# Pool columns of a hybrid layer computed channel by token, in groups of 512 tokens

## The chip, the cores and the metric

One Trainium2 chip, one core in use. The metric is the device time of the program in microseconds (us); lower is better. Every number is a time of an execution on the chip or is read from the trace of one such execution.

## The reference, cut to what matters

One layer on 1024 tokens of width 1024, all float32:

```python
h = rms_norm(x, norm1_g)
u, q, k, v = split(h @ w_in)             # 512 | 512 | 128 | 128 columns
# pool mixer: 4 channel groups of 128, windows 2, 4, 8, 16 tokens
pooled[g] = trailing_mean(u[g], window[g]) - u[g]
a[g] = (pooled[g] @ pool_w[g]) * pool_scale[g]
# attention: 8 query heads, 2 key heads of 64, window of 128 tokens in chunks of 64,
# q and k normed per head, a bias linear in distance, a sink term in the softmax
b = attention(q, k, v)
x = x + concat(a, b) @ w_out
x = x + square(relu(rms_norm(x, norm2_g) @ w_up)) @ w_down
```

## The kernel before, in words

Each engine has its own program, written out by hand, and runs it strictly in its order; engines meet through semaphores. Tokens come in 8 tiles of 128 (t). A float32 matrix product is made of three fp32r products: each operand is split into a rounded high part (ScalarE, `..._high`, `split_...`) and the rest as a low part (VectorE, `..._low`), and `passes` (L1250) issues high x high, high x low and low x high. x comes transposed; the norm's row factor `rinv` is applied later, when a product leaves PSUM, as one scalar per token, since tokens lie on the partitions.

**Input projection.** `project_in(t, ks)` (L1269) takes eight steps k of 128 rows of w_in. In each step the token tile is the stationary operand, and it issues nine matmuls: three of 256 columns (k and v, bank 2), three of 512 (q, bank 3), three of 512 (u, bank 4). In tile 0 each waits for the split of its w_in columns; later ones wait only for bank 2, 3, 4 to have been copied. The w_in rows come as 8 transfers of 640 KB through 6 staging buffers.

**Per tile, after the projection.** ScalarE copies k and v, q and u out (`copy_kv` L637, `copy_q` L647, `copy_u` L654) with `rinv` as scale. GpSimd squares q and k, VectorE sums (`head_sums`), GpSimd takes the inverse root, VectorE norms (`head_norm` L962). TensorE's `transpose_in(t)` (L1322) turns u (four transposes), then q (four) and k (one). The tile `qkv` is single, so `copy_kv(t)` waits for `transpose_in(t-1)`. `evac_u` and `evac_qk` (ScalarE) bring the results to SBUF. GpSimd adds windows over the four groups (`window_sums` L491), VectorE finishes the mean (`pooled` L935), `mix(t)` (L1345) multiplies in plain float32 by pool_w, one matmul per group, `mix_high` and `mix_low` write the halves of a into `xs`, whose x values are no longer needed.

**Attention.** `score(t)` (L1356) writes banks 5 and 6; `softmax_head`, `exponentials`, `softmax_tail` work on VectorE and ScalarE; `transpose_probs(t)` (L1338) writes the transposed probabilities back into banks 5 and 6, `evac_probs` (L682) copies them out in two instructions, and only then may `score(t+1)` write these banks (its wait on `pT_copied`); `attend(t)` (L1373) uses bank 7.

**TensorE's order** (L1389 to L1423): for each t, part of `project_in(t)`, `transpose_in(t-1)`, the rest of `project_in(t)`, `transpose_probs(t-2)`, `mix(t-1)`, `score(t-1)`, `attend(t-2)`. Then `project_out` (L1297) over w_out, eight steps per tile of six matmuls of 512, with the last attention pieces between, `transpose_x` of the second norm, and the MLP (`up`, `down`), whose seven products per block replace eight.

w_out is loaded into the space of w_in's split parts while these fall free, through 5 staging buffers.

Of the kernel before, what the change touches and what calls it, by code (L numbers as in the profile page):

```python
# [11 lines left out]
P = 128  # L12
BANK = 512
# [3 lines left out]
def hybrid_trunk(nc, x, x_T, columns, w_in, pool_w, w_out, norm2_g, w_up, w_down, out):  # L17
# [26 lines left out]
    w_in_k = w_in[0].rearrange("(k p) e -> k p e", p=P)  # L44
    w_out_k = w_out[0].rearrange("(k p) n -> k p n", p=P)
    w_up_k = w_up[0].rearrange("(k p) f -> p k f", p=P)
    w_down_i = w_down[0].rearrange("(j i p) n -> i p j n", i=2, p=P)
    x1_keep = nc.dram_tensor("x1_keep", [NT, P, D], F32, kind="Internal").ap()
    h_keep = nc.dram_tensor("h_keep", [7, NCK, P, HALF], F32, kind="Internal").ap()

    with ExitStack() as ctx:
# [22 lines left out]
        w_in_s = wgt[:, :].rearrange("p (k h e) -> p k h e", k=KT, h=2)  # L74
# [12 lines left out]
        def view(a, words):  # L87
# [3 lines left out]
        UB = HALO + P  # L91
        a_x = take(2 * D)
        a_A = take(2 * D)
        a_B = take(4 * D)
        a_C = take(3 * D)
        a_ws = take(2 * D)
        a_xn = take(D)
        a_bp = take(D)
        a_junk = take(D // 2)
        xT_slot = [view(a_x + i * D, D).rearrange("p (k n) -> p k n", k=KT) for i in range(2)]  # L100
        u_tok = view(a_A, POOL_W)
        qkv = view(a_A + POOL_W, Q_W + KV_W)
        squares = view(a_A + POOL_W + Q_W + KV_W, Q_W + P)
# [3 lines left out]
        u_T = view(b, GROUPS * UB).rearrange("p (g s) -> p g s", g=GROUPS); b += GROUPS * UB  # L107
        win_a = view(b, GROUPS * UB).rearrange("p (g s) -> p g s", g=GROUPS); b += GROUPS * UB
        win_b = view(b, 3 * UB).rearrange("p (g s) -> p g s", g=3); b += 3 * UB
        assert b <= a_B + 4 * D  # L110
        scores = [view(a_C + i * BANK, BANK).rearrange("p (t j) -> p t j", t=PAIRS) for i in range(2)]
        probs_T = [view(a_C + D + i * BANK, BANK) for i in range(2)]
        values = view(a_C + 2 * D, 8 * P).rearrange("p (r c n) -> p r c n", r=4, c=2)
# [3 lines left out]
        pool_map = view(a_bp + BANK, BANK).rearrange("p (g n) -> p g n", g=GROUPS)  # L117
        junk = view(a_junk, D // 2).bitcast(BF16)

        w_in_stage = ([view(a_C + i * IN_W, IN_W) for i in range(2)] + [view(a_A, IN_W)]  # L120
                      + [view(a_B + i * IN_W, IN_W) for i in range(3)])
        w_out_stage = [view(a, D) for a in (a_ws, a_ws + D, a_x, a_x + D, a_xn)]
        W_OUT_SLOT = [0, 1, 2, 3, 4, 0, 1, 4]
        dist = view(a_ws, P)

        resid = ([view(a_x + i * D, D) for i in range(2)] + [view(a_A + i * D, D) for i in range(2)]
                 + [view(a_B + i * D, D) for i in range(4)])
# [37 lines left out]
        KV_B, Q_B, U_B = 2, 3, 4  # L165
        XT_B = [[5, 6], [1, 7]]
        UT_B, QT_B, KT_B = 0, 1, 7
        MIX_B, SC_B, OUT_B = 0, [5, 6], 7
        TOK_B = [2, 3, 4, 0]

# [6 lines left out]
        w_in_in = [sem(f"w_in_in{i}") for i in range(6)]  # L177
        w_out_in = [sem(f"w_out_in{i}") for i in range(5)]
# [4 lines left out]
        d_in = {q: [sem(f"d_in_{q}_{i}") for i in range(8)] for q in ("B11", "B12", "B22", "B21")}  # L183
# [9 lines left out]
        w_in_hi, w_in_lo = sem("w_in_hi"), sem("w_in_lo")  # L193
        rows_hi, rows_lo = sem("rows_hi"), sem("rows_lo")

        in_done = sem("in_done")
        kv_done, q_done = sem("kv_done"), sem("q_done")
        kv_copied, q_copied, u_copied = sem("kv_copied"), sem("q_copied"), sem("u_copied")
# [3 lines left out]
        uT_done, qT_done, kT_done = sem("uT_done"), sem("qT_done"), sem("kT_done")  # L202
        halo_ready, u_T_ready, q_T_ready, keys_ready = sem("halo_ready"), sem("u_T_ready"), sem("q_T_ready"), sem("keys_ready")

        win_step, pool_step, pooled_ready = sem("win_step"), sem("pool_step"), sem("pooled_ready")
        mix_done, mix_hi, mix_lo = sem("mix_done"), sem("mix_hi"), sem("mix_lo")
# [19 lines left out]
        KV_COLS, Q_COLS, U_COLS = slice(POOL_W + Q_W, IN_W), slice(POOL_W, POOL_W + Q_W), slice(0, POOL_W)  # L226
        PIECES = {0: (KV_COLS, Q_COLS, U_COLS), 1: (slice(POOL_W, IN_W), U_COLS)}

        def w_pieces(k):
            return PIECES.get(k, (slice(0, IN_W),))  # L230

        def w_count(k, cols=U_COLS):

            done = sum(len(w_pieces(j)) for j in range(k))
            return done + 1 + min(i for i, c in enumerate(w_pieces(k)) if c.start <= cols.start and cols.stop <= c.stop)
# [57 lines left out]
        def _(sp):  # L293
# [10 lines left out]
            def load_w_in(k):  # L304
                if k >= 6:
                    sp.wait_ge(w_in_lo, w_count(k - 6))
                sp.dma_start(w_in_stage[k % 6], w_in_k[k]).then_inc(w_in_in[k % 6], 16)

            def load_w_out(k):
                slot = W_OUT_SLOT[k]  # L310
                if slot in W_OUT_SLOT[:k]:
                    sp.wait_ge(rows_lo, W_OUT_SLOT.index(slot) + 1)
# [52 lines left out]
            for k in range(6):  # L365
                load_w_in(k)
            load_x(0)
            load_w_in(6)
            load_w_in(7)
            load_xT(1)  # L370
            sp.dma_start(pool_map, pool_w).then_inc(pool_map_in, 16)
            for t in range(1, NT):
                if t + 1 < NT:
                    load_xT(t + 1)
                load_x(t)
            sp.wait_ge(setup_done, 4)
            load_w_out(0)
            load_w_out(1)
            sp.wait_ge(xT_lo, 2 * (NT - 1))
            load_w_out(2)  # L380
            sp.wait_ge(xT_lo, 2 * NT)
            load_w_out(3)
            sp.wait_ge(sumsq_ready, NT)
            load_w_out(4)
            for k in range(5, KT):
                load_w_out(k)
            sp.wait_ge(in_done, KT * NT)
            load_raw(1)
# [12 lines left out]
            for t in range(4, NT):  # L401
                sp.dma_start(resid[t], x_t[ORDER[t]]).then_inc(resid_in[t], 16)
# [63 lines left out]
        def _(pool):  # L466
# [1050 lines left out]
```

## Time and profile before

| | us |
|---|---|
| median of 3 runs | 874.14 (873.89 to 874.4) |
| the profiled execution, its own time | 874.23 |
| its span in the trace | 871.8 |
| TensorE busy | 863.9 |
| VectorE busy | 531.8 |
| ScalarE busy | 418.5 |
| GpSimd busy | 269.9 |

The span runs from the first to the last recorded instruction; the 2.4 us between it and the execution's time lie around it. A matmul's record lasts longer than the distance to the next one, since matmuls overlap in the array: what it costs is the distance of the starts. The part up to the first transpose of the second norm (L1265) ends at 189.56 us of the span.

### The profile page before, as it was taken

Reading aid. Unit: us, or ns where it says so; the run is one execution under the profiler, and the core shown is the slowest. Engines: PE = TensorE matmul, PEld = TensorE weight load, DVE = VectorE, ACT = ScalarE, POOL = GpSimd, SP = SyncE. Lnnn points to the kernel's source line nnn. Section 1 sums busy time; section 2 is a strip of 40 time slices with the busy share of each in tenths; the row PEclk is TensorE's granted clock in tenths of the full one; section 3 lists DMA queues with packets and bytes.
Section 4 is the critical chain, followed back from the end, with each engine's and each line's share of the span. In section 5 each row is a group of like instructions: output and inputs, shape, how many; then the busy total and the mean of one; then the engine's idle time right before and its main releaser. Section 6 shows DMA issues by size and latency. Waiting matters only on the chain.

```text
span 871.8 us, 10957 instructions
## 1 busy us (share of the span) xinstructions
PE 863.9 (99%) x4128; PEld 715.8 (82%) x4128; DVE 531.8 (61%) x800; ACT 418.5 (48%) x746; POOL 269.9 (31%) x202
## 2 busy tenths in 40 slices
PE   8999999999999999999999999999999999999998
PEld 6888888788888888888888888888888888888886
DVE  7666558944458676567666666466945464646462
ACT  7566658632236655555555555444333333333330
POOL 0633444300231342222333222104544004444440
PEclk9999999999999999999999999999999999999999
DMA  8311232452111564444555442889752553242421
GB/s 350 122 49 49 90 105 49 170 180 86 49 48 35 191 194 161 133 134 133 171 178 158 157 133 85 301 319 390 252 184 97 169 193 120 96 147 97 145 97 73
DMA packets 66340, 128.38 MB, mean 147 GB/s; under 512 B 3568, under 2 KB 19952, under 8 KB 66288
## 3 DMA queue, kind: packets, MB, share of 16 engines
q1 hardware_dynamic: 66144, 127.68, 42.6%
q8 instruction: 33, 0.54, 0.2%
q14 instruction: 19, 0.16, 0.1%
q10 hardware_dynamic: 144, 0.01, 0.0%
HBM read 89.92 MB, written 37.75 MB: 146 GB/s over the span
## 4 chain that ended last, share of the span: by engine, by line
PE 89%; DVE 5%; DMA 2%; ACT 2%; POOL 1%; issue 1%; SPq 0%; ACTq 0%; DVEq 0%; POOLq 0%
PE bank L1252 28%; PE bank L1254 28%; PE bank L1253 28%; DMA mem<-in_w_in 2%; PE bank L1367 1%; DVE ring L1033 1%; PE bank L1265 1%; PE bank L1352 1%; PE bank L1382 1%; POOL mem L504 1%; DMA raw<-in_w_up 1%; PE bank L1342 1%; DVE wgt L932 1%; DVE h_set L1065 1%; DVE t_M L1041 1%
## 5 line engine op out<-in xcount | busy, mean ns | idle before, releaser
L1252 PE MATMUL bank<-b_op,s_op 128*128 128x512 f32 x448 | 174.6, 390 | 0.0
L1254 PE MATMUL bank<-b_op,s_op 128*128 128x512 f32 x448 | 174.5, 390 | 0.0
L1253 PE MATMUL bank<-b_op,s_op 128*128 128x512 f32 x448 | 174.5, 390 | 0.0
L572 POOL TENSOR_TENSOR b_sum<-d_raw,d_raw 128x1024 f32<-128x1024 f32 x40 | 97.7, 2442 | 199.8 <-DVE b_op L1076 199.8
L1072 DVE TENSOR_TENSOR s_op<-s_in,s_op 128x1024 fp32r<-128x1024 f32 x56 | 75.0, 1338 | 124.8 <-ACT s_op L775 124.8
L775 ACT ACTIVATE s_op<-s_in 128x1024 fp32r<-128x1024 f32 x56 | 59.4, 1060 | 177.7 <-PE bank L1254 147.1
L1252 PE MATMUL bank<-wgt,xs 128*128 128x256 f32 (+1 forms) x320 | 121.1, 378 | 1.8 <-DVE wgt L926 1.5
L1253 PE MATMUL bank<-wgt,xs 128*128 128x256 f32 (+1 forms) x320 | 118.4, 370 | 0.0
L1254 PE MATMUL bank<-wgt,xs 128*128 128x256 f32 (+1 forms) x320 | 118.3, 370 | 0.0
L1033 DVE TENSOR_TENSOR ring<-raw,ring 128x512 fp32r<-128x512 f32 x96 | 88.8, 938 | 31.0 <-ACT ring L723 29.5
L1252 PE MATMUL bank<-xs,ring 128*128 128x512 f32 x256 | 99.9, 390 | 0.1
L1254 PE MATMUL bank<-xs,ring 128*128 128x512 f32 x256 | 99.8, 390 | 0.0
L1253 PE MATMUL bank<-xs,ring 128*128 128x512 f32 x256 | 99.7, 390 | 0.0
L1252 PEld LDWEIGHTS bank<-b_op,s_op 128*128 128x128 f32 x448 | 84.1, 188 | 17.9 <-DVE b_op L1076 0.4
L1253 PEld LDWEIGHTS bank<-b_op,s_op 128*128 128x128 f32 x448 | 84.1, 188 | 17.4
L1254 PEld LDWEIGHTS bank<-b_op,s_op 128*128 128x128 f32 x448 | 84.1, 188 | 17.3
L538 POOL TENSOR_TENSOR raw<-raw 128x512 f32<-128x512 f32 x16 | 26.2, 1640 | 167.2 <-DVE ring L1033 167.0
L1252 PE MATMUL bank<-t_M,ring 128*128 128x512 f32 x192 | 74.9, 390 | 0.1
L1254 PE MATMUL bank<-t_M,ring 128*128 128x512 f32 x192 | 74.8, 390 | 0.0
L1253 PE MATMUL bank<-t_M,ring 128*128 128x512 f32 x192 | 74.8, 389 | 0.0
L1252 PEld LDWEIGHTS bank<-wgt,xs 128*128 128x128 f32 x320 | 60.3, 188 | 16.4 <-issue 4.0
L723 ACT ACTIVATE ring<-raw 128x512 fp32r<-128x512 f32 x96 | 59.3, 620 | 25.2 <-POOL raw L538 22.7
(129 smaller groups left out, 1358.2 us busy)
## 6 DMA issues: line engine op xcount, KB each, us to landing
s_in<-h_keep SPq DMA_DIRECT2D x56, 512.0 KB, 3.9
h_keep<-h_set SPq DMA_DIRECT2D x16, 1280.0 KB, 5.1
raw<-in_w_up SPq DMA_DIRECT2D x16, 1024.0 KB, 6.4
d_raw<-in_w_down SPq DMA_DIRECT2D x32, 512.0 KB, 7.7
mem<-in_x SPq DMA_DIRECT2D x16, 512.0 KB, 5.7
h_keep<-h_set SPq DMA_DIRECT2D x16, 512.0 KB, 3.8
mem<-in_w_in SPq DMA_DIRECT2D x8, 640.0 KB, 8.0
mem<-in_x_T SPq DMA_DIRECT2D x8, 512.0 KB, 3.8
```

What stands on the lines that cost most here:

```text
L504: nc.gpsimd.tensor_tensor(out=dst[:, d0:d0 + cnt, lo:UB], in0=src[:, s0:s0 + cnt, lo:UB], in1=src[:, s0:s0 + cnt, lo - shift:UB - shift], ...
L538: nc.gpsimd.tensor_tensor(out=w12, in0=w12, in1=w11, op=ALU.subtract).then_inc(w_four_ready, 1)
L572: nc.gpsimd.tensor_tensor(out=b_sum[G % 2], in0=group_rows(qa, g), in1=group_rows(qb, g), op=op).then_inc(b_summed, 1)
L723: nc.scalar.activation(ring[n % 6][:, HI], weight_block(n), ACT.Copy).then_inc(w_hi, 1)
L775: nc.scalar.activation(s_op[G % 3][:, HI], s_in[G % 3], ACT.Copy).then_inc(op_hi, 1)
L932: nc.vector.tensor_tensor(out=w_out_s[:, k, LO, :], in0=w_out_stage[W_OUT_SLOT[k]], in1=w_out_s[:, k, HI, :].bitcast(F32), op=ALU.subtract ...
L1033: nc.vector.tensor_tensor(out=ring[n % 6][:, LO], in0=weight_block(n), in1=ring[n % 6][:, HI].bitcast(F32), op=ALU.subtract).then_inc(w_lo, 1)
L1041: nc.vector.tensor_tensor(out=lo, in0=src, in1=hi.bitcast(F32), op=ALU.subtract).then_inc(t_lo, 1)
L1072: nc.vector.tensor_tensor(out=s_op[G % 3][:, LO], in0=s_in[G % 3], in1=s_op[G % 3][:, HI].bitcast(F32), op=ALU.subtract).then_inc(op_lo, 1)
L1252: nc.tensor.matmul(out_ap, lhs[HI], rhs[HI], start=first, stop=False, skip_group_check=chained)
L1253: nc.tensor.matmul(out_ap, lhs[HI], rhs[LO], start=False, stop=False, skip_group_check=chained)
L1254: return nc.tensor.matmul(out_ap, lhs[LO], rhs[HI], start=False, stop=last, skip_group_check=chained)
```

## The change

The columns of w_in are treated in two parts. The k, v and q columns (768) keep their scheme: `project_qkv(t, ks)`, six matmuls per step. The u columns are computed with the weights as the stationary operand and 512 tokens (h = 0 or 1) as the moving one, one channel group g at a time: `project_u(h, g)`, 24 matmuls of 512 columns, so that u leaves the array already as channel by token. The row factor now lies along the free axis: `rinv` goes through DRAM and comes back as a row on all partitions, and VectorE multiplies by it (`scale_u`). Window sums, mean and mix run per (h, g) on 512 tokens. The pooled values and pool_w are split in high and low parts, and `mix(h, g)` is three fp32r matmuls of 512 columns. u and mix use banks 4 and 0 alternately. w_in arrives as 8 transfers of 384 KB (q, k, v columns) and, behind x and x_T, 4 of 512 KB (u columns); w_out has 3 staging buffers in place of 5.

```diff
             def project_qkv(t, ks):
...
+                    elif first:
                         pe.wait_ge(kv_copied, t)
+                        pe.wait_ge(q_copied, t)
...
+            def project_u(h, g):
+                n = GROUPS * h + g
+                cols = slice(g * P, (g + 1) * P)
+                pe.wait_ge(xT_lo, 2 * KH * (h + 1))
+                if g >= 2:
+                    pe.wait_ge(u_ready, n - 1)
+                elif h:
+                    pe.wait_ge(mix_lo, GROUPS * (h - 1) + g + 3)
+                for k in range(KT):
+                    if n == 0:
+                        pe.wait_ge(w_u_lo, k + 1)
+                    last = passes(bank[U_B[g % 2]][:, :], [w_u_s[:, k, part, cols] for part in (HI, LO)],
+                                  [xs[k // KH, h][:, part, k % KH, :] for part in (HI, LO)], k == 0, k == KT - 1)
+                last.then_inc(u_done, 1)
...
+            def mix(h, g):
+                n = GROUPS * h + g
+                pe.wait_ge(pooled_lo, n + 1)
+                if n == 0:
+                    pe.wait_ge(map_lo, 1)
+                if g < 2:
+                    pe.wait_ge(u_ready, GROUPS * h + g + 3)
+                else:
+                    pe.wait_ge(mix_lo, n - 1)
+                last = passes(bank[U_B[g % 2]][:, :], [pool_map[:, part, cols] for part in (HI, LO)],
+                              [pooled_part(h, g)[:, part, :] for part in (HI, LO)], True, True)
...
 # TensorE's order, one line per stretch; project_qkv(t) whole unless steps are given
+ project_qkv(0)  project_qkv(1)  transpose_in(0)
+ project_qkv(2, 0..3)  score(0)  project_qkv(2, 4..7)  transpose_in(1)
+ project_u(0,0)  project_u(0,1)  transpose_probs(0)  score(1)  attend(0)
+ project_qkv(3)  transpose_in(2)  project_u(0,2)  project_u(0,3)  transpose_probs(1)  score(2)  attend(1)
+ project_qkv(4, 0..3)  mix(0,0)  mix(0,1)  project_qkv(4, 4..7)  transpose_in(3)
+ mix(0,2)  mix(0,3)  transpose_probs(2)  score(3)  attend(2)
+ project_u(1,0)  project_qkv(5)  transpose_in(4)
+ project_u(1,1)  project_u(1,2)  transpose_probs(3)  score(4)  attend(3)
+ project_u(1,3)  project_qkv(6, 0..3)  transpose_in(5)  project_qkv(6, 4..7)
+ transpose_probs(4)  score(5)  attend(4)  project_qkv(7)  transpose_in(6)
+ mix(1,0)  mix(1,1)  project_out(0, 0..2)  mix(1,2)  mix(1,3)
+ transpose_probs(5)  score(6)  attend(5)  project_out(0, 3..5)  transpose_in(7)  project_out(0, 6..7)
+ project_out(1, 0..1)  transpose_probs(6)  score(7)  attend(6)  project_out(1, 2..7)  project_out(2, 0..1)
+ transpose_probs(7)  project_out(2, 2..3)  attend(7)  transpose_x(8)  project_out(2, 4..7)
 # ScalarE's order in the stretches that the prediction walks through
+ split_w_qkv(0..7)  sum_squares_x(0)  x_high(1)  split_w_u(0..3)  copy_kv(0)  copy_q(0)
+ x_high(2)  sum_squares_x(1)  split_w_u(4..7)  evac_qk(0)  copy_kv(1)  copy_q(1)
...
+ x_high(7)  attention_high(0)  evac_probs(1)  sum_squares_x(7)  pooled_high(0,0)  exponentials(2)
+ pooled_high(0,1)  attention_high(1)  mix_high(0,0)  mix_high(0,1)  pooled_high(0,2)  pooled_high(0,3)
+ evac_qk(3)  copy_kv(4)  copy_q(4)  mix_high(0,2)  evac_probs(2)  mix_high(0,3)
...
+ evac_qk(5)  split_w_out(0)  split_w_out(1)  copy_kv(6)  copy_q(6)  split_w_out(2)  evac_probs(4)
+ split_w_out(3)  attention_high(4)  exponentials(5)  pooled_high(1,1)  split_w_out(4)  split_w_out(5)
+ evac_qk(6)  copy_kv(7)  copy_q(7)  mix_high(1,0)
 # VectorE's, likewise
+ place_values(0)  head_sums(0)  x_low(2)  split_w_u(4..7)  head_norm(0)
...
+ scale_u(0,3)  attention_low(0)  softmax_head(2)  pooled_low(0,0)  pooled(0,2)  softmax_tail(2)  pooled_low(0,1)
...
+ softmax_head(5)  split_w_out(3)  attention_low(4)  softmax_tail(5)  pooled(1,3)  pooled_low(1,1)
```

In `pooled_high(1, g)` with odd g ScalarE waits for all eight `pooled`. SyncE loads, in this order: x_T of tile 0, the eight q, k, v parts, x of tile 0, x_T of tile 1, two u parts, x_T of tile 2, x of tile 1, two u parts, x_T of tile 3, x of tile 2, and so on. From `transpose_x` on only the places of some buffers differ, and the third `project_out` has four steps left there in place of five.

## Rows read from the trace of the kernel before

**Rows 1.** Page: busy time per engine, and TensorE's granted clock in 40 slices.
```profile
PE 863.9 (99%) x4128; PEld 715.8 (82%) x4128; DVE 531.8 (61%) x800; ACT 418.5 (48%) x746; POOL 269.9 (31%) x202
PEclk9999999999999999999999999999999999999999
```
**Rows 2.** Page: the chain that ended last, shares of the span by engine.
```profile
PE 89%; DVE 5%; DMA 2%; ACT 2%; POOL 1%; issue 1%; SPq 0%; ACTq 0%; DVEq 0%; POOLq 0%
```
**Rows 3.** Waits of TensorE past tile 0: total us, times, longest.
```profile
PE bank L1332 <- DVE mem L966: 0.6, 1, 0.6
PE bank L1342 <- DVE mem L1003: 0.4, 1, 0.4
```
**Rows 4.** Timeline of TensorE, first 50 us: start, duration, instruction, count.
```profile
1.55 4.88 PE L1388 MATMUL bank<-mem 128*128 128x128 f32 x24 [1.55 <-POOL mem L471]
7.49 0.35 PE L1252 MATMUL bank<-wgt,xs 128*128 128x256 f32 x1 [1.06 <-DVE wgt L926]
...
23.52 0.28 PE L1252 MATMUL bank<-wgt,xs 128*128 128x256 f32 x1
...
25.31 0.28 PE L1252 MATMUL bank<-wgt,xs 128*128 128x256 f32 x1
...
27.05 0.28 PE L1252 MATMUL bank<-wgt,xs 128*128 128x256 f32 x1
...
30.54 0.60 PE L1328 MATMUL bank<-mem 128*128 128x128 f32 x4
30.98 0.60 PE L1332 MATMUL bank<-mem 128*128 128x128 f32 x4
...
38.49 1.05 PE L1352 MATMUL bank<-mem 128*128 128x128 f32 x8
39.47 1.16 PE L1367 MATMUL bank<-mem 64*128 64x128 f32 x16
```
**Rows 5.** Timeline of all engines, 130 to 137 us, same columns.
```profile
131.52 1.04 PE L1342 MATMUL bank<-mem 128*128 128x128 f32 x8
...
132.16 1.09 ACT L687 ACTIVATE mem<-bank 128x512 f32<-128x512 f32 x2 [0.45 <-PE bank L1342]
...
132.40 1.06 PE L1352 MATMUL bank<-mem 128*128 128x128 f32 x8
```
**Rows 6.** Timeline of ScalarE, 14 to 19 us.
```profile
14.10 1.37 ACT L624 ACTIVATE wgt<-mem 128x1280 fp32r<-128x1280 f32 x1 [0.23 <-DMA mem<-in_w_in]
...
16.95 1.37 ACT L624 ACTIVATE wgt<-mem 128x1280 fp32r<-128x1280 f32 x1 [1.49 <-DMA mem<-in_w_in]
```
**Rows 7.** Groups of ScalarE by form, 0 to 210 us: busy, mean ns | idle before.
```profile
L705 ACT ACTIVATE mem<-mem 128x128 f32<-128x128 f32 x64 | 25.0, 391 | 15.2 <-DVE mem L987 15.2
...
L587 ACT ACTIVATE mem<-mem 128x1024 bf16<-128x1024 f32 x11 | 11.5, 1049 | 12.6 <-DVE mem L1024 9.5 <-DMA mem<-in_x 3.1
L600 ACT ACTIVATE xs<-mem 128x512 fp32r<-128x512 f32 x16 | 9.2, 617 | 2.2 <-DMA mem<-in_x_T 2.2
...
L631 ACT ACTIVATE wgt<-mem 128x1024 fp32r<-128x1024 f32 x8 | 8.1, 1056 | 1.0 <-DMA mem<-in_w_out 1.0
...
L650 ACT ACTIVATE mem<-bank,mem 128x512 f32<-128x512 f32 x8 | 5.5, 687 | 0.4
...
L644 ACT ACTIVATE mem<-bank,mem 128x256 f32<-128x256 f32 x8 | 3.8, 472 | 19.6 <-PE bank L1254 18.9 <-POOL mem L488 0.7
...
L679 ACT ACTIVATE mem<-bank,mem 128x128 f32<-128x128 f32 x8 | 2.9, 367 | 0.0
...
L624 ACT ACTIVATE wgt<-mem 128x512 fp32r<-128x512 f32 x3 | 2.0, 708 | 0.0
```
**Rows 8.** Groups of VectorE by form, 0 to 210 us.
```profile
L1003 DVE TENSOR_SCALAR mem<-mem 128x128 f32<-128x128 f32 x64 | 14.1, 283 | 0.6
...
L985 DVE TENSOR_REDUCE mem<-mem 128x4 f32<-128x512 f32 x16 | 11.0, 686 | 0.6
...
L983 DVE TENSOR_TENSOR mem<-bank,mem 128x512 f32<-128x512 f32 x14 | 9.6, 685 | 3.4 <-PE bank L1367 3.4
```

More of the change, by code:

```diff
@@ new lines, in _ @@
+            exponentials(3)
+            evac_qk(4)
+            copy_kv(5)
+            copy_q(5)
+            evac_probs(3)
+            attention_high(3)
+            exponentials(4, (0,))
+            pooled_high(1, 0)
+            exponentials(4, (1,))
+            evac_qk(5)
+            for k in range(2):
+                split_w_out(k)
+            copy_kv(6)
+            copy_q(6)
+            split_w_out(2)
+            evac_probs(4)
+            split_w_out(3)
+            attention_high(4)
@@ new lines, in _ @@
+            exponentials(5)
+            pooled_high(1, 1)
+            for k in range(4, 6):
+                split_w_out(k)
+            evac_qk(6)
+            copy_kv(7)
+            copy_q(7)
+            mix_high(1, 0)
+            mix_high(1, 1)
+            pooled_high(1, 2)
+            pooled_high(1, 3)
+            split_w_out(6)
+            evac_probs(5)
+            mix_high(1, 2)
+            mix_high(1, 3)
+            attention_high(5)
+            exponentials(6, (0,))
+            split_w_out(7)
@@ new lines, in _ @@
+            scale_u(1, 0)
+            place_values(5)
+            head_sums(5)
+            head_norm(5)
+            scale_u(1, 1)
+            pooled(1, 0)
+            scale_u(1, 2)
+            softmax_head(4)
+            attention_low(3)
+            softmax_tail(4)
+            pooled(1, 1)
+            scale_u(1, 3)
+            pooled_low(1, 0)
+            pooled(1, 2)
+            for k in range(2):
+                split_w_out(k)
+            place_values(6)
+            head_sums(6)
@@ new lines, in _ @@
+            split_w_out(2)
+            head_norm(6)
+            softmax_head(5)
+            split_w_out(3)
+            attention_low(4)
+            softmax_tail(5)
+            pooled(1, 3)
+            pooled_low(1, 1)
+            for k in range(4, 6):
+                split_w_out(k)
+            place_values(7)
+            head_sums(7)
+            mix_low(1, 0)
+            mix_low(1, 1)
+            pooled_low(1, 2)
+            pooled_low(1, 3)
+            head_norm(7)
+            split_w_out(6)
@@ new lines, in _ @@
+            mix(0, 0)
+            mix(0, 1)
+            project_qkv(4, range(KH, KT))
+            transpose_in(3)
+            mix(0, 2)
+            mix(0, 3)
+            transpose_probs(2)
+            score(3)
+            attend(2)
+            project_u(1, 0)
+            project_qkv(5, range(KT))
+            transpose_in(4)
+            project_u(1, 1)
+            project_u(1, 2)
+            transpose_probs(3)
+            score(4)
+            attend(3)
+            project_u(1, 3)
```

735 lines of the change are left out of this document (430 added, 305 removed).

## The prediction

> **What bounds the kernel now.** Read the page first: TensorE is busy in 99% of the span, the next engine in 61%, and the granted clock is full in every slice [rows 1]. The chain of waits agrees: 89% of it is TensorE [rows 2]. TensorE's waits past the first tile come to 0.6 and 0.4 us [rows 3]. So the time is TensorE's own work, and an edit is worth what it takes out of TensorE's queue, less each wait that it puts there. In the timeline a tile's projection is 15 units of 256 columns per step; from 25.31 to 27.05 that is 1.74 us, 0.116 us a unit, 0.232 us for a matmul of 512 [rows 4]. The profiled execution (874.23) is the median of the runs (874.14); the sum is made on it, and the 2.4 us around the span stay.
>
> **TensorE's work.** Removed: the u transposes, four in 0.44 us per tile (30.54 to 30.98), 8 x 0.44 = 3.5; the float32 mix, 0.98 us per tile (38.49 to 39.47), 8 x 0.98 = 7.8 [rows 4]. The two old waits go with the order, 1.0 [rows 3]. Added: 8 mixes of three matmuls of 512, 24 x 0.232 = 5.6. The u product is 192 matmuls of 512 columns before and after; weights instead of tokens as the stationary operand change no count of columns. It could stream a little better or worse (I hold 0.005 us each, 1 us in all, for both ends) and I take 0. Together: -3.5 - 7.8 + 5.6 - 1.0 = **-6.7 us**.
>
> **Start: weights in two parts.** Before, tile 0 ends at 23.52 [rows 4] for 8 x 1.74 = 13.9 of work: it lags its work by 9.6. In the new order `project_qkv(1)` waits for `copy_q(0)`, and ScalarE comes to this only behind four splits of u weights. Loads: between 14.10 and 16.95 x (512 KB) and w_in's step 6 (640 KB) land, 404 KB per us; by 14.10, 4352 KB have landed [rows 6]. Two u parts are complete after 512 + 8 x 384 + 4 x 512 = 5632 KB, so at 14.1 + 1280/404 = 17.3. Then two splits (0.7 each, less overlap: 18.6), `copy_kv` 0.47, `copy_q` 0.69 [rows 7]: 19.8. By then TensorE has done 8 x 1.04 = 8.3 of work, finished near 16.2, and stands for 3.6. It lags by 11.5 instead of 9.6: **+1.9**. Ends: -1.8 (no stand at all), +4 (the loads drop to the bandwidth of smaller rows).
>
> **After `project_qkv(1)`.** `transpose_in(0)` follows at once, then `project_qkv(2)`, which needs banks 2 and 3 copied. ScalarE can copy only after `evac_qk(0)`: 0.69 (a copy of 512 columns from PSUM, as `copy_q`) + 0.37, then 0.47 + 0.69 [rows 7], with a handover 2.2 us in which TensorE has nothing. Before, u's matmuls and the steps behind `transpose_in` covered this. **+2.2** (1.5 to 3.5: `head_norm(0)` on VectorE now stands behind four u splits, and by my count is ready just as it is asked for).
>
> **Transposed probabilities.** This is the largest term. `transpose_probs` starts at 131.52 and frees TensorE at 132.40; ScalarE's two copies run from 132.16 to 133.25 [rows 5]. Before, `mix` (0.98) fills exactly that gap, and `score` starts when the copies are done. In the new order `score(t)` stands directly behind `transpose_probs(t-1)` in all seven places, t = 1 to 7, and the banks are the same. Each waits 133.3 - 132.4 = 0.9 to 0.95: **+6.6**. Ends: 5.5 and 8. This takes back nearly all of the saved work by itself.
>
> **Waits from the order of ScalarE and VectorE.** I walked the new queues with the durations of [rows 7, 8].
> - `score(3)`: ScalarE has `evac_qk(3)`, both copies and `mix_high(0,2)` ahead of `evac_probs(2)`, 0.7 beyond the 0.95. `score(5)`: `copy_q(6)` can't start before `project_qkv(6)` ends, and `split_w_out(2)` (1.0) comes before `evac_probs(4)`: 1.1 beyond. Together 1.8.
> - `mix(0,1)` needs `pooled_low(0,1)`, which VectorE does behind `softmax_head(2)` (two heads of 1.7: an add of 0.69, a maximum of 0.69, two small ones) [rows 8], `pooled_low(0,0)`, `pooled(0,2)` and `softmax_tail(2)` (two of 1.2, mostly four multiplies of 0.28, with ScalarE's eight exponentials of 0.39 between). This takes some 8.2 from the end of `score(2)`; TensorE is there after `attend(1)`, four steps and a mix, 1.0 + 4.2 + 0.7 = 5.9. Wait 2.5.
> - `mix(1,1)` needs `pooled_high(1,1)`, behind `exponentials(5)` and `pooled(1,3)`: 2.0. Then ScalarE still has two `split_w_out` of 1.0, `evac_qk(6)` and two copies, 1.0 + 1.2, before `project_out(0)` may write banks 2 and 3: 4.2 from `pooled_high`, of which low part and mix cover 1.5: 2.7.
>
> That is 9.0 at full count; the lower end is 0 (each off-by-one in such a walk shortens a wait, and records on one engine overlap by 0.05 to 0.1, as two copies of 0.60 in 1.09 show [rows 5]), the upper 12. I take **+6.5**, nearer to the walk.
>
> **Cost nothing.** `scale_u`, `pooled`, the low and high parts on 512 tokens: the elements per engine hardly change, and ScalarE loses 32 small `mix_high` and all `copy_u`; these engines are idle 39 to 52% of the span [rows 1]. `rinv` by DRAM: needed by `scale_u(0,0)`, whose first reader on TensorE's side is `project_u(0,2)`, some 18 us after `project_u(0,0)`; it would need over 10 us for both transfers to be late. SyncE waits in it before x_T of tile 4, whose high part ScalarE does just before `evac_probs(0)`; that has about 3 us to spare. w_out in 3 buffers: `project_out(0)` reaches step 3 after the attention pieces, and steps 6 and 7 have two w_out splits behind `softmax_head(6)`; ready about when asked for, 0 to 2 us. From `transpose_x` on TensorE is as full as before, so the delay goes through to the end one for one.
>
> **Sum.** -6.7 + 1.9 + 2.2 + 6.6 + 6.5 = +10.5: 874.2 + 10.5 = **884.7 us**.
>
> **The clock.** The granted clock is 1.00 all through [rows 1]. But the first 24 transposes, after TensorE had done nothing, take 4.88/24 = 0.20 us each, and later ones 0.11 [rows 4], a ratio near that of 1.2 to 2.4 GHz. The trace of before has no later stand of over 1.1 us; the new order has one of 3.6 and several of 2 to 3. Whether the array falls back there no row shows. If it does once, and is slow for as long as at the start, from 1.55 to about 7.5, with half the rate, it costs up to 3 us. The Trainium skill ("TensorE: Matmul & The Clock Gate", the part on the HAM clock gate) says that an idle stretch sends the array back to 1.2 GHz and that activity must release it again. By that rule the second tile would start slowly, and the sum would be about 887 to 888. It is a rival below.
>
> **Rivals.**
> 1. Forecast, 884.7, own range 880 to 889: chance 0.62.
> 2. Only the structural waits (start, first transposes, seven copies) are real and the order of ScalarE and VectorE costs nothing: -6.7 + 1.9 + 2.2 + 6.6 = +4.0, 878.2. For it: both engines have idle time. Against it: the idle time is not where the chains above stand. Chance 0.16.
> 3. The clock falls in the stand at 16 to 20 us, and perhaps at a later one: 884.7 + 3 = 888. For it: the first 24 transposes. Against it: no row shows a fall after work has begun. Chance 0.12.
> 4. Faster, by one mechanism: ScalarE is never late, at tile 0 too. Then `copy_q(0)` is done when `project_qkv(0)` ends (start -1.8 instead of +1.9), the copies after `transpose_in(0)` are what remains, with the seven bank copies: with -6.7 - 1.8 + 2.2 + 6.6 = +0.3 it is a draw; if the evacuation of q and k also comes early enough to halve the 2.2, and the copies of the transposed probabilities cost 0.7 instead of 0.95, it is -6.7 - 1.8 + 1.1 + 4.9 = -2.5, 871.7. It decides at a sum of all waits of 6.7. Against it: the loads alone bring the u parts at 17.3. Chance 0.07 for faster, 0.03 for the draw.
>
> No run of this kernel differs from the median by over 0.03%; 0.2% (1.7 us) is about what can be told. Slower holds 0.90, same 0.03, faster 0.07. The range takes in rival 2's upper part and rival 3: 877 to 890.
>
> **What would show it.** In the profile after: TensorE's share falls from 99% to about 97%, its matmul work by some 6 us; the start of the second `project_qkv` near 20 us, behind ScalarE's copy; seven waits of about 0.9 at the `score` matmuls on `evac_probs`, 6 us or more in all; waits of 2 to 3 us at `mix(0,1)`, `mix(1,1)` and the first `project_out`; the first transpose of the second norm near 201 to 202, with four steps left behind it. Wrong would be: `score` without a wait; the second tile starting before 18 us; u matmuls at starts other than 0.23 apart; or a part behind `transpose_x` that is not as long as before.

## The result and the profile after

The changed kernel takes 902.6 us (median of 5 runs, 901.4 to 902.8) against 874.14: a ratio of 1.0323, with a 95% interval of 1.0311 to 1.0335. It is slower by 28.5 us. I had forecast slower, but by 10.5, and 902.6 lies far outside 877 to 890.

Page of the kernel after: span, busy time of each engine, then TensorE's busy tenths and granted clock in 40 slices of 22.5 us [before: rows 1], then the chain by engine [rows 2].

```profile
span 900.6 us, 10790 instructions
...
PE 868.0 (96%) x4056; PEld 715.8 (79%) x4056; DVE 544.4 (60%) x779; ACT 408.0 (45%) x714; POOL 267.1 (30%) x190
...
PE   7989799799999999999999999999999999999998
...
PEclk9899899899999999999999999999999999999999
...
PE 83%; DVE 6%; DMA 5%; ACT 3%; issue 2%; POOL 1%; SPq 1%; ACTq 0%; DVEq 0%; POOLq 0%
```

Nearly all of it is in the first ten slices. The first transpose of the second norm was at 189.56 before, with one step more of `project_out` left behind it (1.38 us); now it is at 218.98. That is +28.0, and the rest of the kernel is as long as it was to within 0.8 us. Two things show in the first slices: TensorE is not busy, and its clock is under nine tenths in three of them. I call a time in which TensorE waits with nothing to do a stand. TensorE's waits, which were 0.6 and 0.4 past tile 0 [rows 3], are now:

```profile
PE bank L1596 <- ACT mem L756: 10.5, 7, 3.9
PE bank L1474 <- DVE pooled_odd L1101: 8.7, 2, 5.3
PE bank L1474 <- ACT mem L722: 5.3, 2, 3.3
...
PE bank L1562 <- DVE xs L1171: 0.6, 1, 0.6
```

L1596 is `score` behind `evac_probs`, L1101 is `pooled_low`, L722 and L716 are `copy_q` and `copy_kv`. In the experiments below the line numbers are shifted by one to three. The long ones, and some of the short ones, in TensorE's timeline (start, duration, instruction, [idle before it]):

```profile
20.09 0.36 PE L1474 MATMUL bank<-wgt,xs 128*128 128x256 f32 x1 [3.33 <-ACT mem L722]
...
32.83 0.35 PE L1474 MATMUL bank<-wgt,xs 128*128 128x256 f32 x1 [2.02 <-ACT mem L722]
...
60.55 1.16 PE L1596 MATMUL bank<-mem 64*128 64x128 f32 x16 [3.94 <-ACT mem L756]
...
98.69 0.80 PE L1474 MATMUL bank<-pooled_odd,pool_map 128*128 128x512 f32 x1 [5.26 <-DVE pooled_odd L1101]
...
139.10 1.16 PE L1596 MATMUL bank<-mem 64*128 64x128 f32 x16 [0.83 <-ACT mem L756]
...
158.69 1.16 PE L1596 MATMUL bank<-mem 64*128 64x128 f32 x16 [1.91 <-ACT mem L756]
...
174.93 0.80 PE L1474 MATMUL bank<-pooled_odd,pool_map 128*128 128x512 f32 x1 [3.39 <-DVE pooled_odd L1101]
177.92 0.76 PE L1474 MATMUL bank<-wgt,xs 128*128 128x512 f32 x1 [1.34 <-ACT mem L716]
```

TensorE in the stretches of 5 us with less than the full clock (stretch, busy us, granted clock, DMA share, GB/s).

```profile
20.00:25.00 5.00, 4.91 (x20) 0.66 0.99 368
30.00:35.00 5.00, 2.98 (x18) 0.93 0.01 2
35.00:40.00 5.00, 5.00 (x31) 0.73 0.31 107
60.00:65.00 5.00, 4.45 (x29) 0.66 0.51 186
95.00:100.00 5.00, 1.31 (x3) 0.57 0.00 0
100.00:105.00 5.00, 5.00 (x24) 0.74 0.28 17
170.00:175.00 5.00, 1.10 (x5) 0.92 0.39 105
175.00:180.00 5.00, 3.66 (x8) 0.50 0.46 114
180.00:185.00 5.00, 5.00 (x21) 0.89 0.63 204
```

Each of the five stands of 2.0 us and more has a stretch of low clock behind it. The shorter ones (one of 1.91 at 158.69 is the longest) start none; the one of 1.34 at 177.92 lies in the stretch behind 174.93. In such a stretch the array runs at the lower of its two levels, 1.2 GHz instead of 2.4: after the stand at 20.09 the matmuls of 512 come 0.43 apart instead of 0.23.

```profile
20.83 0.63 PE L1475 MATMUL bank<-wgt,xs 128*128 128x512 f32 x1
21.26 0.63 PE L1476 MATMUL bank<-wgt,xs 128*128 128x512 f32 x1
```

### The profile page after: what moved, and what is told of

The parts are those of the page before. It is cut to its first block, busy times and chain, and to the rows that moved or that the text cites. A ratio compares the mean times of both kernels' runs of the same rounds, so it can differ in the third digit from the quotient of the medians.

```text
span 900.6 us, 10790 instructions
## 1 busy us (share of the span) xinstructions
PE 868.0 (96%) x4056; PEld 715.8 (79%) x4056; DVE 544.4 (60%) x779; ACT 408.0 (45%) x714; POOL 267.1 (30%) x190
## 4 chain that ended last, share of the span: by engine, by line
PE 83%; DVE 6%; DMA 5%; ACT 3%; issue 2%; POOL 1%; SPq 1%; ACTq 0%; DVEq 0%; POOLq 0%
PE bank L1474 27%; PE bank L1476 27%; PE bank L1475 27%; DMA rinv_keep<-mem 1%; DMA mem<-in_w_in 1%; DMA d_raw<-in_w_down 1%; DVE ring L1186 1%; PE bank L1596 1%; PE bank L1613 1%; PE bank L1487 1%; DMA raw<-in_w_up 1%; DVE mem L1157 1%; DMA mem<-in_x_T 1%; DVE h_set L1218 1%; ACT mem L756 0%
## 5 line engine op out<-in xcount | busy, mean ns | idle before, releaser
L1474 PE MATMUL bank<-wgt,xs 128*128 128x512 f32 (+1 forms) x256 | 98.3, 384 | 7.1 <-ACT mem L722 5.3
L1476 PEld LDWEIGHTS bank<-b_op,s_op 128*128 128x128 f32 x448 | 84.1, 188 | 17.4
L1475 PE MATMUL bank<-wgt,xs 128*128 128x512 f32 (+1 forms) x256 | 95.8, 374 | 0.0
L1476 PE MATMUL bank<-wgt,xs 128*128 128x512 f32 (+1 forms) x256 | 95.4, 372 | 0.0
L1474 PEld LDWEIGHTS bank<-wgt,xs 128*128 128x128 f32 x256 | 50.3, 196 | 19.6 <-issue 8.5
```

The costliest lines, as they stand in the source:

```text
L1474: nc.tensor.matmul(out_ap, lhs[HI], rhs[HI], start=first, stop=False, skip_group_check=chained)
L1475: nc.tensor.matmul(out_ap, lhs[HI], rhs[LO], start=False, stop=False, skip_group_check=chained)
L1476: return nc.tensor.matmul(out_ap, lhs[LO], rhs[HI], start=False, stop=last, skip_group_check=chained)
```

## The experiments

The theory after this reading: three causes, (a) waits made by the order of the four engines' programs, (b) the clock behind the long ones, (c) at `score(1)` a wait that comes from the DMA of `rinv`. The rival to (a) and (b): the kernel lacks engine time in this stretch, and a wait that is taken away comes back elsewhere. All ratios are against the kernel before.

### e1_fill: the clock alone

```diff
+            fill(28)   # transposes of the identity into an idle bank, ahead of project_qkv(1);
+                       # 16 ahead of project_qkv(2), 34 of score(1), 46 of mix(0,1), 28 of mix(1,1)
```

> The changed kernel, with idle transposes of the identity (0.11 us each) put into TensorE's queue in five stands: 28 before the second project_qkv, 16 before the third, 34 before score(1), 46 before mix(0,1), 28 before mix(1,1). Nothing else moves. Theory (stands are doubled by the clock: each of the five stands of over 2 us is followed by some 3 to 5 us at half rate, about 9 us lost in all): the granted clock stays at 1.00 but for the last stand of 1.3 us, and the time falls by 6 to 9 us, to 893.5 to 896.5. Rival (the slow stretches cost nothing, since TensorE would only wait longer at the next stand): the same time, 901 to 903. Rival 2 (the fillers delay real work): slower.

Measured: 896.09, 1.0247 (1.0233 to 1.0261), 6.5 us less than the changed kernel with no wait taken away. That is inside the theory's range. The granted clock is 1.00 to 150 us and 0.97 from there to 200, where one stand of 2.03 was left. So the falls of the clock cost at least 6.5 us, and they come from TensorE standing still.

### e2_xT4: one load ahead of rinv's transfers

SyncE's issues in the kernel after, then ScalarE: `rinv` goes out at 40.68, and nothing behind it is issued until 52.05.

```profile
40.68 0.38 SPq L337 DMA_DIRECT2D rinv_keep<-mem  x1
52.05 0.33 SPq L344 DMA_DIRECT2D mem<-rinv_keep  x1
52.42 0.43 SPq L322 DMA_DIRECT2D mem<-in_x_T  x1
...
58.28 1.15 ACT L662 ACTIVATE xs<-mem 128x512 fp32r<-128x512 f32 x2 [11.63 <-DMA mem<-in_x_T]
```

It is 2 KB in pieces of 4 bytes, and SyncE waits 10.9 us for it. The DMA engines are all but idle meanwhile: 0 GB/s from 40 to 45 and 3 from 45 to 50. x_T of tile 4 is queued behind, ScalarE's `x_high(4)` (L662) needs it and waits 11.63 for it, and `evac_probs(0)` comes behind `x_high(4)`.

```diff
             load_x(3)
+            load_xT(4)
             turn_rinv(0)
```

> The changed kernel, with the load of x_T tile 4 issued before SyncE waits for the row factors' way through DRAM (10.9 us). Theory (the wait of 3.9 us at score(1) is that load, since ScalarE does its high part just before evac_probs(0)): the wait falls to the 0.9 of the other copies, the clock does not fall there, and the time falls by 3 + about 1.7, to 898. Rival (score(1) waits for the copies or for q in any case): the wait stays over 3 us and the time within 1 us of 902.6.

Measured: 896.49, 1.0254 (1.024 to 1.0268), 6.1 less, against 4.7 expected. `score(1)` now waits as long as the others:

```profile
57.03 1.16 PE L1598 MATMUL bank<-mem 64*128 64x128 f32 x16 [0.83 <-ACT mem L758]
```

The stand is shorter by 3.1; the clock behind it is full again. The spans of the two profiles differ by 5.7: 3.1 of idle time and 2.6 of TensorE's busy time (868.0 to 865.4), with the same matmuls. One line costs a fifth of the loss.

### e3_low01: a wait moved

```diff
-            exponentials(2)
             pooled_high(0, 1)
+            exponentials(2)
...
+            pooled_low(0, 1)
             pooled(0, 2)
             softmax_tail(2)
-            pooled_low(0, 1)
```

> The changed kernel, with pooled_high(0,1) before exponentials(2) on ScalarE and pooled_low(0,1) before pooled(0,2) and softmax_tail(2) on VectorE. Theory (the wait of 5.3 us at mix(0,1) is VectorE's order): the wait goes, with the slow clock behind it, 5.3 + 1.5 us; transpose_probs(2) may then wait up to 2 us for softmax_tail(2), which is 0.7 later and asked for 5 us earlier: 896 to 899. Rival (the chain over exponentials decides, and the wait moves as a whole to mix(0,2), transpose_in(3) or transpose_probs(2)): 901 to 903.

Measured: 902.92, 1.0326 (1.0311 to 1.0342): nothing gained. The 5.26 at `mix(0,1)` is gone, but the groups behind it now wait:

```profile
100.92 0.33 PE L1562 MATMUL bank<-mem 128*128 128x128 f32 x1 [0.56 <-DVE xs L1171]
102.83 0.50 PE L1474 MATMUL bank<-pooled_even,pool_map 128*128 128x512 f32 x1 [1.58 <-DVE pooled_even L1101]
105.19 0.80 PE L1474 MATMUL bank<-pooled_odd,pool_map 128*128 128x512 f32 x1 [1.39 <-DVE pooled_odd L1101]
```

These are 3.5 of the 5.3, and `score(1)` waited 1.1 longer in this profile. The clock lost more, too: it was 0.50 and 0.55 from 105 to 115, where the kernel after had it full again. The time is the rival's; the wait moved for the most part, not as a whole.

### e4_adds: VectorE beside GpSimd

Why is `pooled_low(0,1)` so late? VectorE and GpSimd in the kernel after:

```profile
92.57 4.79 POOL L551 TENSOR_TENSOR mem<-mem 128x527 f32<-128x527 f32 x4 [6.54 <-DVE mem L1094]
92.75 2.36 DVE L1157 TENSOR_SCALAR mem<-mem 128x128 f32<-128x128 f32 x4
95.03 1.01 DVE L1151 TENSOR_TENSOR mem<-mem 128x4 f32<-128x4 f32 x1
...
96.29 1.74 DVE L1157 TENSOR_SCALAR mem<-mem 128x128 f32<-128x128 f32 x4
```

L1157 are the four multiplies of `softmax_tail`, which take 0.87 together when GpSimd is still; L1151 is an add of 4 columns, else 0.16. GpSimd's window adds of group 3 run just then. VectorE's instructions that read a bank keep their 0.69 beside such adds (L1081 and L1171 from 84.40 to 85.77, with adds from 81.99 to 86.04).

```diff
                 for shift in shifts of group 3, from the second on:
+                    end = lo + 8        # instead of all 512 tokens
```

> The changed kernel, but in the window sums of group 3 of the first half, the last three of four adds do only 8 of 512 tokens: this leaves out part of the pool mixer, and is meant for its time alone. GpSimd's stretch from 92.6 to 97.4 falls to about 1.4 us. Theory (VectorE's multiplies of softmax_tail(2) take 4 in 2.36 and 1.74 us instead of 0.87, because GpSimd adds at the same time): they return to 0.87 to 0.95, mix(0,1) waits some 2.5 to 3 us instead of 5.3, and the time falls by 2 to 3.5 us, to 899 to 900.5. Rival (the long multiplies have another cause, or the wait is set by the exponentials on ScalarE): the multiplies stay long or the time stays within 1 us of 902.6.

This kernel leaves out most of the last three window adds of group 3, and only its time is of use.

Measured: 897.88, 1.027 (1.0256 to 1.0284), 4.7 less, more than the theory's 2 to 3.5. The same rows:

```profile
91.54 2.10 POOL L552 TENSOR_TENSOR mem<-mem 128x527 f32<-128x527 f32 x4 [6.50 <-DVE mem L1095]
91.72 1.56 DVE L1158 TENSOR_SCALAR mem<-mem 128x128 f32<-128x128 f32 x4
...
93.63 0.88 DVE L1158 TENSOR_SCALAR mem<-mem 128x128 f32<-128x128 f32 x4
...
95.16 0.79 PE L1475 MATMUL bank<-pooled_odd,pool_map 128*128 128x512 f32 x1 [2.75 <-DVE pooled_odd L1102]
```

With GpSimd's adds down from 4.79 to 2.10, the same VectorE work shrank by 2.5 and the stand at `mix(0,1)` from 5.26 to 2.75. So some of VectorE's instructions on SBUF are slowed by GpSimd's adds, and this makes about half of that stand. The Trainium skill has the rule ("SBUF — State Buffer", the part on the two separate sides): the two engines share one pair of ports, and whichever gets it keeps it for the whole instruction; of VectorE's instructions this concerns those in a mode that takes two ports and those with two inputs in SBUF. The rows agree in that the add of two SBUF inputs grew by 0.85, which is less than one of GpSimd's adds (4.79 for four), and that instructions with one input in a bank didn't grow. In which mode the multiplies run no row shows.

### e5_between, e6_start: work into the gaps

e5 is e2 with a piece of TensorE's own work between `transpose_probs` and `score` in all seven places, as `mix` lay there before, and `evac_probs` earlier on ScalarE. e6 is the changed kernel with the first copies ahead of the u splits on ScalarE, `head_norm(0)` ahead of the last four u splits on VectorE (and the first four behind `head_sums(0)`), `transpose_in(0)` ahead of the last step of `project_qkv(1)`, and the wait for `copy_q` behind the k and v matmuls.

```diff
             # e5, one place of seven
             project_u(0, 0)
+            transpose_probs(0)
             project_u(0, 1)
-            transpose_probs(0)
             score(1)
             # e6, ScalarE
+            copy_kv(0)  copy_q(0)
             for k in range(4): split_w_u(k)
-            copy_kv(0)  copy_q(0)
             # e6, TensorE
-            project_qkv(1, 0..7)  transpose_in(0)
+            project_qkv(1, 0..6)  transpose_in(0)  project_qkv(1, 7)
```

> The kernel of e2_xT4 (896.5), with TensorE's own work put between transpose_probs(t-1) and score(t) in all seven places (one project_u, two mixes, one step of project_qkv or of project_out), and evac_probs ahead of attention_high(0), of copy_kv(4), of copy_kv(6) and of split_w_out(6) on ScalarE. Theory (each score waits for the two copies of the probabilities, 0.83 each and up to 1.9 where ScalarE is late, 7.4 in all): these waits go, 896.5 - 7 = 889 to 891. Rival (the waits only move to the next stands, mix(0,1), mix(1,1) and the first project_out, since VectorE's and ScalarE's chains set the pace there): 893 to 896.

Measured: 893.69, 1.0223 (1.0209 to 1.0237), 2.8 less than e2, in the rival's range. No `score` waits any more, which were 7.4 us of stands in e2; about half of them are back at other places (`transpose_in(3)` 2.60 where it was 0.62, `project_u(1,0)` 1.38, an `attend` 0.5).

> The changed kernel, with copy_kv(0) and copy_q(0) ahead of the four splits of u weights, transpose_in(0) before the last step of project_qkv(1), head_norm(0) ahead of four u splits, and the wait for q's copy moved behind the k and v matmuls. Theory (the stands of 3.3 and 2.0 us at the start are ScalarE's order, and each makes the clock fall): the second project_qkv starts near 18, both stands shrink to about 1.3, and with the slow stretches behind them (1.7 and 1.3 us) the time falls by 4.5 to 6.5, to 896 to 898. Rival (the stand is the landing of x and x_T behind the weights, so that the copies can't be earlier): 900 to 902.6.

Measured: 899.45, 1.0286 (1.0272 to 1.03), 3.2 less than the changed kernel, short of the 4.5 to 6.5 of the theory. The second tile starts at 17.4 instead of 20.09, and the stands of the start are 0.2, 0.5 and 0.4. But TensorE comes to `score(1)` 6.8 earlier (49.78 instead of 56.61), and its start, which hangs on the load behind `rinv`'s transfer, moves by only 3.4 (57.16 instead of 60.55):

```profile
57.16 2.08 PE L1597 MATMUL bank<-mem 64*128 64x128 f32 x16 [7.38 <-ACT mem L756]
```

So (c) took back half of what TensorE had gained by then.

### e7_order, e8_order2, e9_order3: all of it together

e7 is e2, e5 and e6 and a new order around the mixes. e8 and e9 each take the stands that the last one left, and reorder there. The main edits:

```diff
+            # e7: mix(0,0), mix(0,1) behind step 5 of project_qkv(4); both pooled_high ahead of
+            # exponentials(2), both pooled_low ahead of softmax_tail(2); pooled(1,1..3) earlier
+            # e8: transpose_probs(1) behind project_u(0,3); attention_low(4) ahead of softmax_head(5)
+            # e9: attention_low(0) ahead of x_low(7); copies of tile 7 between the halves of
+            # exponentials(5); attention_low(5) ahead of softmax_head(6); w_out splits into idle time
```

> e2, e5 and e6 together, and a new order around the mixes: project_qkv(4) does six steps before mix(0,0) and mix(0,1); pooled(0,2) before softmax_head(2), so that GpSimd's adds for group 3 run before softmax_tail(2); the high and low parts of pooled(0,1) ahead of the exponentials; pooled(1,3) ahead of place_values(6), and the high part of pooled(1,1) ahead of exponentials(5); transpose_in(6) before the last two steps of project_qkv(7), and its copies before two splits of w_out. Theory (the new form of the u columns saves TensorE 6 us, and all of the loss is the order of the queues and the clock): no stand of over 1.5 us, the clock at 1.00, and a time below before: 868 to 874. Rival (ScalarE, VectorE and GpSimd have not the time for the chains on 512 tokens, in whatever order): stands move, 878 to 890.

Measured: 882.22, 1.0092 (1.0078 to 1.0105), 20.4 less than the changed kernel, though in the rival's range (878 to 890): most of the waits are the order's. Left are 4.96 at `transpose_in(6)`, 3.00 at `attend(1)`, 1.40 at `project_u(1,0)` and 1.33 at `mix(1,2)`.

> e7_order with its remaining stands taken on: one step of project_qkv(4) in place of project_u(0,3) between transpose_probs(1) and score(2), so that attend(1) need not wait 3.0 for the low part of attention(0); two steps of project_qkv(5) before project_u(1,0) (1.4); attention(4)'s high and low part ahead of pooled(1,1) and of softmax_head(5) (5.0 at transpose_in(6)); the split of w_out row 5 behind the pooled parts (1.3). Theory (order and clock are all of the loss): 882.2 less 10.7 of stands less 3 to 4 of slow clock, 867 to 871, faster than before by up to 7. Rival (the chains of VectorE and GpSimd on 512 tokens are too long, and the stands come back elsewhere): 876 to 882.

Measured: 881.37, 1.0079 (1.0065 to 1.0093), no clear gain, in the rival's range. The stands of 4.96, 1.40 and 1.33 went, the 3.00 at `attend(1)` is 2.25; 3.38 at `transpose_in(7)`, 1.83 at `project_out(0)` and 0.91 at `mix(1,1)` came.

> The changed kernel with e8_order2's orders and four more edits, one for each stand of over 0.5 us that e8_order2 still shows behind the start: attention_low(0) ahead of x_low(7) on VectorE (2.25 at attend(1)); pooled_low(1, 1) and the third split of w_out ahead of head_norm(6) (0.91 at mix(1, 1)); copy_kv(7) and copy_q(7) between the two halves of exponentials(5) (1.83 at project_out(0)); attention_low(5) ahead of softmax_head(6), with the splits of w_out in VectorE's idle time before head_norm(7) (3.38 at the k of transpose_in(7)). On TensorE one step more of project_out(0) stands ahead of transpose_probs(5), and two more of project_out(1) ahead of transpose_probs(6), since the probabilities come later than TensorE would. Theory (what is over is waits that the order makes, and the clock falls only behind the long ones): 8.4 of stands and 2 to 3 of slow clock go: span 880 - 8.4 - 2.5 = 869, time 870 to 872, the first time below the kernel before (874.1, ratio about 0.997). Rival (VectorE and ScalarE have no slack there, a stand taken away comes back at the next place): like e7_order to e8_order2, where 3.5 of stands went and 0.9 of the time: 878 to 880, ratio over 1.004.

Measured: 881.69, 1.0089 (1.0075 to 1.0103), no gain: this is the rival, even a little above its 878 to 880. The four stands went, and these took their place:

```profile
84.88 0.80 PE L1477 MATMUL bank<-pooled_even,pool_map 128*128 128x512 f32 x1 [3.40 <-DVE pooled_even L1104]
...
172.81 0.50 PE L1477 MATMUL bank<-wgt,xs 128*128 128x512 f32 x1 [4.17 <-DVE wgt L1073]
```

The second waits for the last w_out split (L1073). VectorE does it behind `softmax_head(6)`, in e8 too; with the 3.38 at `transpose_in(7)` gone, TensorE is there before it.

### b1_mixfirst: the copies in the kernel before

The opposite test of one term: the kernel before, with nothing changed but `mix` moved out of the gap between `transpose_probs` and `score`, behind the loop for the last tile too.

```diff
+                if t >= 1:
+                    mix(t - 1)
                 if t >= 2:
                     transpose_probs(t - 2)
                 if t >= 1:
-                    mix(t - 1)
                     score(t - 1)
```

> The kernel before, with mix(t-1) issued ahead of transpose_probs(t-2) in place of behind it, in all seven places: score stands directly behind the transposes, as in the changed kernel, and nothing else differs. Theory (mix covered ScalarE's two copies of the probabilities): seven waits of 0.8 to 0.95 at score, 874.2 + 5.6 to 6.6 = 880 to 881. Rival (a wait so short is taken up by TensorE's queue, or the copies come earlier): 874 to 875.

Measured: 880.67, 1.0073 (1.006 to 1.0085), +6.5. Its waits of TensorE:

```profile
PE bank L1367 <- ACT mem L687: 5.8, 7, 0.8
...
PE bank L1352 <- DVE mem L945: 1.6, 2, 1.2
```

L1367 is `score` there, L1352 `mix`. Seven waits of 0.83 make 5.8 of the 6.5. The rest comes with the edit too, but elsewhere: the last `mix`, now earlier, waits 1.19 for `pooled`, another 0.4, and the old waits of 0.6 and 0.4 [rows 3] are gone.

### e10_order4, e11_order5: VectorE's idle time and GpSimd's adds

e10 puts VectorE's late work into stretches in which e9's rows show it idle. e11 moves `pooled(0,2)`, which releases the group's adds on GpSimd.

```diff
+            # e10: x_low(7) ahead of head_norm(3); mix_low(1,2), mix_low(1,3), attention_low(5)
+            # ahead of head_norm(7); the last w_out split ahead of softmax_head(6);
+            # softmax_head(2), pooled_low(0,0) ahead of pooled(0,2); add_x1(0) ahead of softmax_head(7)
             # e11
             softmax_head(2, first head)
+            pooled(0, 2)
             softmax_head(2, second head)
             pooled_low(0, 0)
-            pooled(0, 2)
             pooled_low(0, 1)
+            attention_low(1)
             softmax_tail(2)
-            attention_low(1)
```

> The changed kernel with e9_order3's orders, and the work that VectorE did late there moved into the idle time that its rows show: x_low(7) before head_norm(3) (VectorE stood from 70.7 to 72.6 there, and the two instructions of x_low took 2.65 us later beside GpSimd's adds, against 1.28); softmax_head(2) and pooled_low(0, 0) ahead of pooled(0, 2); mix_low(1, 2), mix_low(1, 3) and attention_low(5) before head_norm(7) (idle from 163.3 to 165.4); the last split of w_out before the exponentials and softmax_head(6); add_x1(0) before softmax_head(7). TensorE takes two more steps of project_out(1) ahead of transpose_probs(6). Theory (orders with fewer stands exist, each found where an idle stretch of VectorE takes the late work): the stands of 3.40 at mix(0, 0), 4.17 at project_out(0) and 1.20 at project_out(2) go, with 2.5 of slow clock behind the first two: 880 - 8.8 - 2.5 = 869, time about 870 to 872, below the kernel before (874.1). Rival (in these stretches VectorE itself is the bound, so that what stands goes to the next place): 877 to 882 as in the two runs before.

Measured: 875.33 (11 runs), 1.0012 (1.0003 to 1.0021), 6.4 less than e9, between theory and rival. Here is what remained, VectorE beside the adds, then the stand and the clock (a stretch of 5 us):

```profile
81.64 5.12 POOL L553 TENSOR_TENSOR mem<-mem 128x527 f32<-128x527 f32 x4 [3.63 <-DVE mem L1096]
...
83.28 2.35 DVE L1159 TENSOR_SCALAR mem<-mem 128x128 f32<-128x128 f32 x4
...
88.55 0.33 PE L1565 MATMUL bank<-mem 128*128 128x128 f32 x1 [2.77 <-DVE xs L1173]
```

```profile
90.00:95.00 5.00, 4.23 (x18) 0.50 0.40 22
```

> e10_order4 with one more edit on VectorE: pooled(0, 2), which releases the last group of GpSimd's window adds, between the halves of softmax_head(2), and attention_low(1) ahead of softmax_tail(2). In e10_order4 the adds ran from 81.64 to 86.8, and softmax_tail(2) beside them took 5.9 us (82.0 to 87.9; softmax_tail(5) with no adds about 2.6); behind it the k of transpose_in(3) stood for 2.77 us, mix(0, 2) for 1.01, and the granted clock was 0.50 from 90 to 95 and 0.81 from 95 to 100. Theory (contention with GpSimd's adds makes this stand, and the stand makes the slow clock): the adds run from about 79 to 84, beside the half of softmax_head that works on a bank and only the first part of softmax_tail; the stand falls to under 1, the clock stays at 1.00, and of 2.8 + 1.0 + 3.4 us 5 to 7 go: time 868 to 871, ratio 0.994 to 0.997, below the kernel before. Rival (the adds cost VectorE the same wherever they are): the stand comes at transpose_probs(2) or at mix(0, 2) instead, 2 to 3 us, with the clock's fall: 873 to 876.

Measured: 873.45 (11 runs, 872.7 to 874.4), 0.9992 (0.9983 to 1.0001). This is 1.9 less than e10, not the 5 to 7 of the theory. The time lies in the rival's range (873 to 876), but the rival's sign, a stand of 2 to 3 us with a fall of the clock, isn't there: the granted clock is 1.00 throughout in the profile. The multiplies beside no adds take 0.88 again:

```profile
78.91 5.02 POOL L553 TENSOR_TENSOR mem<-mem 128x527 f32<-128x527 f32 x4 [1.32 <-DVE mem L1096]
79.40 0.69 DVE L1141 TENSOR_REDUCE mem<-mem 128x4 f32<-128x512 f32 x1
...
81.25 1.55 DVE L1103 TENSOR_TENSOR pooled_even<-mem,pooled_even 128x512 fp32r<-128x512 f32 x1
82.72 1.76 DVE L1103 TENSOR_TENSOR pooled_odd<-mem,pooled_odd 128x512 fp32r<-128x512 f32 x1
...
85.41 0.88 DVE L1159 TENSOR_SCALAR mem<-mem 128x128 f32<-128x128 f32 x4
```

But now `pooled_low`, a subtraction of two SBUF inputs, lies beside the adds, 1.55 and 1.76 instead of 0.68, and the mixes wait 1.28 and 0.71 for it. The maximum (L1141), which has one input and reads SBUF as well, keeps its 0.69 beside the same adds: it isn't all work on SBUF that is slowed. Its page:

```profile
span 871.2 us, 10789 instructions
...
PE 859.7 (99%) x4056; PEld 707.8 (81%) x4056; DVE 549.2 (63%) x779; ACT 408.6 (47%) x714; POOL 268.0 (31%) x190
```

So the changed kernel in a better order is as fast as the one before, with the same work as its first version: the difference of 29 us between the two versions is order, clock and one transfer. It is not measurably faster than the kernel before: TensorE's busy time is 4.2 shorter (859.7 against 863.9), its idle time 3.6 longer (11.5 against 7.9).

## Why the prediction was wrong

The kernels after and e11 issue the same matmuls, one with a falling clock and one with a full one. With the kernel before [rows 1] their pages split the span's +28.8: TensorE's work at full clock 859.7 - 863.9 = -4.2; slow clock 868.0 - 859.7 = +8.3; TensorE idle (900.6 - 868.0) - (871.8 - 863.9) = +24.7. My sum had -5.7, 0 and +16.2.

- **The clock, failed.** The sum had nothing for it. It stood as a rival, once, at up to 3 us, with a chance of 0.12. It fell five times, four of them behind stands that the sum itself contained, the fifth behind the 3.94 at `score(1)`, of which the sum had 0.9. e1 shows 6.5 of it with an edit that touches nothing else; busy times say 8.3. The argument "no row shows a fall after work has begun" failed: the trace of before had no stand as long as those that I predicted, so it could not show one.
- **`rinv` by DRAM at no cost, failed.** I wrote that it "would need over 10 us for both transfers to be late" and that `evac_probs(0)` had about 3 us to spare. The first transfer alone held SyncE for 10.9 (9.2 in e2, 10.2 in e6). It cost 3.1 of stand, 6.1 in time (e2), and took back half of what e6 had gained. Why 2 KB take so long no run tests.
- **Order of ScalarE and VectorE, mis-sized: +6.5 taken.** Measured in its places: `mix(0,1)` 5.26 (walk 2.5), `mix(1,1)` 3.39 (2.0), `project_out(0)` 1.34 (2.7), `score(3)` and `score(5)` together 1.5 over the 0.83 (1.8), and 0.6 at a place that I hadn't seen: 12.1, where the walk had 9.0. The shading from 9.0 to 6.5 was wrong, and the walk itself used mean durations of VectorE: four multiplies at 4 x 0.283 = 1.13 [rows 8], which take 0.87 alone and took 2.36 and 1.74 beside GpSimd's adds. e4 shows the adds to make about half of the largest stand.
- **Seven bank copies, right in mechanism, 0.7 too much.** 0.83 to 0.94 in each, what else was late left out, 5.9 in all where +6.6 was forecast; b1 shows 5.8 of such waits in the kernel before.
- **The start, right.** Second `project_qkv` at 20.09 (19.8 forecast), the wait after `project_qkv(1)` 2.02 (2.2). e6 shows that 2.7 of the first was order, and not the loads.
- **TensorE's work, right in sign, 1.5 too much.** -4.2 instead of -5.7. The u matmuls come 0.23 apart, as said. I haven't traced the 1.5.
- **Behind `transpose_x`, right:** the same length to within 1 us.

The error of 18.3 us is thus 8.3 clock, about 8.5 idle time (3.1 `rinv`, 5.6 the order, the rest small and of both signs, the copies' -0.7 among them) and 1.5 work.

## What to carry to other kernels

When a change leaves the bounding engine standing, price two things together: each stand, and the slow clock behind those of about 2 us or more (here 6.5 to 8.3 us for five of them). Walk every queue for what is merely behind a slow instruction, a small scattered transfer on SyncE too, and do not shade a walk that found waits: in an in-order program they are real, and one taken away comes back at the next place until the order as a whole is right (e3, e9). An edit that saves 4 us of matmul time can be worth nothing even after many reorderings; the seven gaps that `mix` had filled were worth 5.8 by themselves.

## What was not expected of the hardware

- The granted clock fell behind every stand of 2.25 us or more in the traces of all these kernels. Between 1.8 and 2.03 it went either way: 1.91 was followed by a fall in e4 and not in the kernel after, 2.02 by one there and not in e2. No single stand of 1.4 or less had one, but in e3 two of 1.58 and 1.39 that lay 2.4 apart did.
- Some of VectorE's instructions on SBUF take much longer while GpSimd adds: four multiplies 2.36 instead of 0.87, an add of 4 columns 1.01 instead of 0.16, a subtraction of 512 columns 1.76 instead of 0.68. Those with an input in a bank and a maximum with one SBUF input keep their time (0.69).
- The issuing queue waited 10.9 us for 2 KB written to DRAM in pieces of 4 bytes, with the DMA engines at 0 to 3 GB/s. The second such store, issued at 99.97 with loads of w_out right behind it, took about as long: `rinv` was loaded back at 111.98.
